# Attention steps of a hybrid decoder kernel: where the causal mask products stand among the score products

## What is computed

```python
kpos = top_idx[..., None] * SEL_BLOCK + jnp.arange(SEL_BLOCK)
ms = sel_ok[..., None] & (kpos <= t[None, None, :, None, None])
ssel = jnp.einsum("bhgqd,bhqnkd->bhgqnk", qb, kg).astype(f32)
ps = masked_softmax(ssel, ms[:, :, None], (-2, -1))
...
mw = (wpos[None, :] <= t[:, None]) & (wpos[None, :] > t[:, None] - WINDOW) & (wpos[None, :] >= 0)
sw = jnp.einsum("bhgqd,bhkd->bhgqk", qb, kwb).astype(f32)
pw = masked_softmax(sw, mw, -1)
...
o = gb[..., 0:1] * o_c + gb[..., 1:2] * o_s + gb[..., 2:3] * o_w
```

## Time and profile before

| | us |
|---|---|
| median of 3 runs | 1338.39 |
| the runs | 1335.49, 1338.39, 1341.69 |
| span of the profiled execution, first to last instruction | 1341.1 |
| attention steps in it, first scores to last transposes | about 711 to 926 |

### The profile page before, as it was taken

The page is one execution under the profiler, slowest core; times in us unless marked ns, Lnnn a source line. Parts: engine busy times, 40 slices in busy tenths (PEclk is TensorE's granted clock), DMA queues, the critical chain, the costliest instruction groups (busy, mean ns, idle before and its releaser), DMA issues. The chain is left out here.

```text
span 1341.1 us, 17990 instructions
## 1 busy us (share of the span) xinstructions
PE 1239.1 (92%) x6572; PEld 960.2 (72%) x6572; DVE 1035.7 (77%) x1161; ACT 774.3 (58%) x1034; POOL 284.3 (21%) x324
## 2 busy tenths in 40 slices
PE   4999999599999999799998999999959999999996
PEld 3877767477777777569866777766747777777772
DVE  6788858789999998567746666653687999989876
ACT  3423224377777777553544565566246777777762
POOL 0112222100000000328004555544140000000022
PEclk8999999699999999899998999999979999999998
DMA  9878973699999999913852333133448999999973
GB/s 356 302 270 318 320 274 110 225 364 398 387 398 378 406 389 377 366 54 128 231 150 79 102 111 109 51 126 125 177 173 312 404 389 393 391 389 391 387 267 137
DMA packets 111951, 359.22 MB, mean 268 GB/s; under 512 B 8049, under 2 KB 16477, under 8 KB 111851
## 3 DMA queue, kind: packets, MB, share of 16 engines
q1 hardware_dynamic: 89992, 282.10, 57.5%
q0 software_dynamic: 17296, 60.38, 12.6%
q10 hardware_dynamic: 4594, 15.84, 2.9%
HBM read 329.94 MB, written 25.21 MB: 265 GB/s over the span
## 5 line engine op out<-in xcount | busy, mean ns | idle before, releaser
L1430 DVE TENSOR_TENSOR w_lo<-raw,w_hi 128x2048 fp32r<-128x2048 f32 x189 | 433.4, 2297 | 48.2 <-ACT w_hi L1424 46.3
L1424 ACT ACTIVATE w_hi<-raw 128x2048 fp32r<-128x2048 f32 x189 | 362.3, 1918 | 78.5 <-PE bank L239 77.1
L237 PE MATMUL bank<-w_lo,xe_hi 128*128 128x512 f32 x512 | 212.3, 415 | 1.1 <-DVE xe_lo L1385 1.1
L239 PE MATMUL bank<-w_hi,xe_hi 128*128 128x512 f32 x512 | 204.1, 399 | 0.0
L238 PE MATMUL bank<-w_hi,xe_lo 128*128 128x512 f32 x512 | 204.1, 399 | 0.0
L227 ACT ACTIVATE w_hi<-raw 128x2048 fp32r<-128x2048 f32 x37 | 70.6, 1911 | 113.4 <-PE bank L239 83.7
L1342 POOL DMA_INDIRECT xg<-scratch_u,tok x32 | 31.4, 982 | 481.8 <-PE bank L1353 456.6
L2673 POOL TENSOR_SCALAR prob<-prob,rsum,gates 128x512 f32<-128x512 f32 (+3 forms) x128 | 108.5, 862 | 91.7 <-DVE rsum L2641 91.7
L237 PE MATMUL bank<-u_lo,w_hi 128*128 128x512 f32 x288 | 119.3, 414 | 8.7 <-DVE q L2338 4.2
L237 PEld LDWEIGHTS bank<-w_lo,xe_hi 128*128 128x128 f32 x512 | 97.4, 190 | 29.9 <-issue 7.9
L238 PE MATMUL bank<-u_hi,w_lo 128*128 128x512 f32 x288 | 115.6, 402 | 0.0
(11 more groups left out here) (351 smaller groups left out, 2283.8 us busy)
## 6 DMA issues: line engine op xcount, KB each, us to landing
raw<-in_w_gu_dram SPq DMA_DIRECT2D x128, 1024.0 KB, 7.8
raw<-in_w_down_dram SPq DMA_DIRECT2D x64, 1024.0 KB, 6.8
ada<-in_ada_w_dram POOLq DMA_DIRECT2D x48, 512.0 KB, 5.7
ada<-in_ada_w_dram SPq DMA_DIRECT2D x32, 512.0 KB, 3.8
scratch_y<-ye ACTq DMA_DIRECT2D x30, 512.0 KB, 7.4
raw<-in_conv_w_in_dram SPq DMA_DIRECT2D x12, 1024.0 KB, 14.6
mod_w<-in_ada_w_dram SPq DMA_DIRECT2D x8, 1024.0 KB, 14.1
raw<-in_w_kv_dram SPq DMA_DIRECT2D x6, 1024.0 KB, 6.9
```

Source lines behind the costliest of these rows:

```text
L237: nc.tensor.matmul(o, lh, rl, start=start, stop=False)
L239: return nc.tensor.matmul(o, lh, rh, start=False, stop=stop)
L1424: nc.scalar.activation(w_hi[:, hslot, :], raw[:, slot, :], ACT.Copy).then_inc(hi_done, 1)
L1430: nc.vector.tensor_tensor(w_lo[:, slot, :], raw[:, slot, :], w_hi[:, hslot, :].bitcast(F32), ALU.subtract).then_inc(lo_done, 1)
```

## The change

`scores_pe` no longer issues the masks of an ordinary unit, nor the signal `att_s` for it. A new function `masks_pe` issues both, and `attention_pe` calls it for u and u+1 after the scores of both. The bank is cleared by the unit's first product alone, and the last mask ends the unit.

```diff
+                m.then_inc(att_s, 1)
             else:
-                for br, i, c0 in PIECES[kind]:
+                for n_, (br, i, c0) in enumerate(PIECES[kind]):
                     w = (i + 1) * P
                     q = q2[:, g % 2, hh_, i * P:(i + 1) * P]
-                    nc.tensor.matmul(o[:, c0:c0 + w], q, k2[:, g, br, 0:w], start=True, stop=False)
-                    nc.tensor.matmul(o[:, c0:c0 + w], q, k2[:, g, 2 + br, 0:w], start=False, stop=False)
-                    m = nc.tensor.matmul(o[:, c0 + i * P:c0 + w], identb[:], causal[:], start=False, stop=True)
+                    nc.tensor.matmul(o[:, c0:c0 + w], q, k2[:, g, br, 0:w], start=(n_ == 0), stop=False,
+                                     skip_group_check=True)
+                    nc.tensor.matmul(o[:, c0:c0 + w], q, k2[:, g, 2 + br, 0:w], start=False, stop=False,
+                                     skip_group_check=True)
+
+        def masks_pe(pe, u):
+
+            g, hh_, kind, n = unit(u)
+            o = bank[u % 3]
+            for br, i, c0 in PIECES[kind]:
+                m = nc.tensor.matmul(o[:, c0 + i * P:c0 + (i + 1) * P], identb[:], causal[:], start=False,
+                                     stop=(br, i, c0) == PIECES[kind][-1], skip_group_check=True)
             m.then_inc(att_s, 1)
...
                 for u in units_of(s):
                     scores_pe(pe, u)
+                for u in units_of(s):
+                    if not is_cmp(u):
+                        masks_pe(pe, u)
```

## The result

The change makes the kernel slower by a small amount: median 1344.89 us over 15 runs (1340.11 to 1349.36) against 1338.39 us over 15 runs of the kernel before (1333.01 to 1343.35). The ratio is 1.0043, 95% interval [1.0029, 1.0057]. By the ratio the loss is 5.8 us, by the medians 6.5.

What follows compares the result with a forecast made beforehand. PE's own issue order was taken to bound most of a step, with a loop through DVE, ACT and POOL catching up in places. Losses of 0.7 + 0.3 + 0.2 = +1.2 us on the median 1338.39 gave 1339.6; range 1333.5 to 1345.0.

Steps and rivals of the forecast that it cites:

- the rival in which masks in a row are not cheaper: Masks in a row cost 0.12 us each, PE loses 1.8 us of its own, and the kernel takes 1342.5; chance 0.10.
- its own sign of being wrong: First scores of the compressed units drifting earlier by 0.5 us or more a group, or later by more than 1 us.
- the loop: DVE, ACT and POOL bring a 0.42 to 0.51 us later release back to PE; as pace-setting rival 1347.2, chance 0.07.
- the clock: Rival: the new order adds or drops a slow-clock stretch of 1.7 us, giving 1336.7 or 1341.3; chance 0.09.
- the price of a mask inside: A mask within scores of 512 columns costs PE 0.12 us; directly behind another mask 0.065 was taken.
- the length added to the query chain: From kind 3's scores to the query products at j = 5, groups 0 to 2: 0.51 us longer.
- The forecast waits of the second halves: Kind 2's transposes in the kind 3 step wait for POOL; second halves together lose 0.3 us.
- the bookkeeping of a first half group: PE's shift followed through kinds 0 to 4: each first half ends 0.24 us later, three times 0.7 us.
- D: PE's shift on entry to a half group of kinds 0 to 4, later counted as positive.
- POOL's slack for the results of kind 2: In the kind 3 step, POOL's end at 810.77 to the second unit's transposes at 811.01: 0.24 us.
- The last group: No query products but ACT's copies: 0.2 us put for its half groups, between -0.8 and +1.5.
- PE's own saving: Masks moved out of the scores free 8.8 us, 88 masks in a row cost 5.7: 3.1 us saved.

Runs made afterwards that it cites:

- Experiment 1: Kernel before, no product moved; only the signal releasing DVE on a step's first unit moved to the second unit's last score product: ratio 1.0050.
- experiment 3: The change made only in the steps of kinds 0, 1 and 2, kinds 3 and 4 as in the kernel before: ratio 1.0023.
- experiment 2: The change made only in the steps of kinds 3 and 4, kinds 0 to 2 as in the kernel before: ratio 1.0052.
- experiment 4: The changed kernel with each unit's masks behind its own scores, ahead of the second unit's scores: ratio 0.9991 to the kernel before.
- experiments 6 to 8: Query products of j = 5 moved behind transposes and values, in the kernel before, the changed one, and with masks behind own unit's scores: 0.9989, 1.0040, 0.9987.

## Why the prediction was right in kind and short in size

The value was +1.2 us and the loss is 5.8 to 6.5 us. That the median still falls inside the range is luck: the upper end was put there for the rival in which masks in a row are not cheaper (1342.5 and a margin), and the trace excludes that rival. By its own sign of being wrong the prediction fails: measured from one compressed unit's mask to the next the second, the third and the last group grew by more than 1 us each (table below); the loop and the clock share in that.

**Right.** That PE would save and the loop would take it back and more; the price of a mask inside (0.12 us) and in a row (0.06 measured, 0.065 taken); the length added to the query chain (0.54, forecast 0.51); waits of "about 2.0" us on the query halves (2.09, 2.08); more and longer waits for POOL (5.2 us and 11 times against 3.3 and 7); DVE's waits for the mask (20.5 us, "18 or more"). The forecast waits of the second halves stand where they were put: 0.44 us at 808.74 and 0.45 at 866.46, forecast 0.40, and 1.24 at 751.15 where 0.54 stood before.

**The step that failed** is the bookkeeping of a first half group: "kind 3's scores started at D - 0.275, and its query chain, 0.51 longer, ends at D + 0.24". I had checked POOL's slack for the results of kind 2 only. The results of kind 1 have as little: before, POOL ends them at 777.77 + 2.49 = 780.26, and PE's second four transposes start at 780.03 + 0.44 = 780.47. Kind 1's release comes 0.46 us later, which is more than the 0.21 us between the two, so PE has to wait there, in the step of kind 2 and ahead of kind 3's scores. The changed kernel shows it at 776.65 (0.49 us) and at 834.51 (0.49 us). The two delays then stand one behind the other instead of side by side: the scores of kind 3 start at D - 0.055 + 0.46 - 0.21 = D + 0.19, the query chain ends at D + 0.70. With the corrected step a group with query products costs about 0.8 us by the sum, not 0.26, and the whole is near +3 us instead of +1.2.

The rows bear this step out. From kind 1's first score product to kind 3's, in the second and third group, it is 7.63 or 7.64 us in the three profiles of before and 8.09 to 8.13 in the three of after: 0.47 longer, where the prediction has 0.22 less and the corrected step 0.25 more. Experiment 1 has 8.11 and 8.12, experiment 3 8.13 and 8.10; experiment 2, with kinds 0 to 2 in the old order, has 7.64, and experiment 4 has 7.59. The rest of the 0.47 is mostly in the slack, which the prediction read too large by the same amount at kind 2 (0.24 us). In each of three places where the transposes wait, they start 0.14 us behind POOL's end (776.51 to 776.65 after, 755.13 to 755.27 and 796.89 to 797.03 before). Of the 0.21 us only 0.07 were free, which makes it 0.39. The listed idle of 0.49 us hides this, since it counts from the last result of the products before; by their spacing of 0.11 us the second four would have started at 776.00, 0.65 us earlier than they did.

**The term left as a rival** is the clock. I gave it 0.09 and took it as luck in either direction. Behind the query waits it comes with the longer waits and has one sign. (Its two times were also counted from different starts, 1336.7 from the median before and 1341.3 from the forecast; from the forecast the lower one is 1337.9.) Its size I can only estimate. The slow stretch from 786.6 to 790.0 lost 1.7 us of full clock, and the one behind the third wait as much, 3.4 us in all. A part of that is waited for anyway. The steps of kind 4 and of the kind 0 behind it (j = 5 and 6) take 13.6 us together in the second group of the three profiles of before, and 14.4 in experiment 3, which has the slow stretch behind a wait that grew by only 0.02 us: 0.8 us. In the third group they take 12.8 us, and 14.3 in experiment 4, with the stretch behind a wait of 1.45 us: 1.5 us. Together that is 2.3 us.

The lengths of the groups (from the compressed unit's mask to the next one's, the last group to the output projection) show where the whole loss lies:

| group | before, three profiles, us | after, three profiles, us | difference of the means |
|---|---|---|---|
| first | 56.7, 56.7, 58.2 | 57.5, 57.5, 58.0 | 0.4 |
| second | 54.9, 54.9, 55.7 | 57.6, 57.6, 57.7 | 2.4 |
| third | 53.4, 53.6, 53.6 | 56.2, 56.2, 56.2 | 2.7 |
| last | 56.3, 56.8, 56.9 | 58.1, 58.1, 58.1 | 1.5 |

The 58.2 and 55.7 us are those of the first profile, which has one more slow stretch in each of these two groups than its repetitions. The changed kernel has the stretch of the second group, right behind the compressed unit, in all three profiles; it is worth 0.8 us. So the loop takes about 1 us in each of the first three groups, the clock 2.3 us behind the query waits and up to 0.8 us behind the second compressed unit. **The last group is the third term that was too small**: 0.2 us in the sum, between -0.8 and +1.5, and 1.5 us by the profiles.

**What stays open.** PE's own saving wasn't measured apart. To the first transpose the steps of kinds 1, 2 and 3 are shorter by 0.08, 0.20 and 0.12 us, more than forecast (0.055, 0.165, 0.055); but in the steps of kinds 1 and 3 looked at the eight transposes then took 1.12 and 1.14 us instead of 1.04, which gives much of it back. Whether these are waits too short to be listed, I didn't try. In the second halves the saving arrives: in the first three groups the step of kind 1 takes 4.52 to 4.55 us instead of 4.60 to 4.62, and that of kind 2 4.04 or 4.05 instead of 4.24. The last group's extra waits on ACT (1.0 us) came with kinds 0 to 2, as experiments 2 and 3 show (2.5 and 3.2 us), and the 0.6 us at the output projection with kinds 3 and 4 (0.8 us in experiment 2, 0.2 in experiment 3), but I didn't follow their chains. Nor did I follow what decides about the slow stretch behind the second compressed unit.

The page "TensorE: Matmul & The Clock Gate" of the Trainium skill (Back-to-back issue gap) has 81 ns for a pair of load and product of 128 columns. The masks in a row ran at 0.06 us here, so the trace decides for the lower figure, for bf16 weights that are the same 128 columns each time.

## What to carry to other kernels

A cheaper order on the busiest engine can be worth nothing, or less, where it delays the signal that feeds a loop back to that engine: move the signal first, alone, and look at the time. When a delay has several places to come back, check the slack at each of them, and ask of every two whether they stand side by side or one behind the other. Count the slack to the start that really follows a signal: here 0.14 us lay between POOL's end and the transposes that had waited for it. Grouping within the unit that is signalled showed no cost (0.9991), and no gain that can be told from none.

## What the runs showed of the hardware that I had not expected

TensorE's clock fell to its lower level behind idle gaps of only about 2 us (0.50 to 0.57 over the next 3 us, six of six in the changed kernel), stayed at 1.00 behind gaps of 1.41 us in the same place (six of six in the kernel before), and stayed up when 24 small bf16 products filled most of the gap (two of two). The gap alone doesn't decide: the clock held behind gaps of 2.11 us (experiment 2) and 2.20 us (experiments 6 to 8), and fell behind gaps of 1.43 and 1.45 us (experiments 3 and 4). Masks of 128 bf16 columns ran 0.06 us apart although each has its own weight load.
